# The low parts of the second layer's weights move from VectorE to GpSimd

## The reference

```python
h = x @ b_w_in[0]                                   # 1024 -> 2560
q, k, v, q_mem = jnp.split(h, [768, 1536, 2304], axis=-1)
mix = moba_attention(...)                           # 12 heads of 64, causal; one block of 256 here
mem_out = memory_cross_attention(q_mem, mem, w_mem_kv[i])
sub = jnp.concatenate([mix, mem_out], axis=-1) @ w_mix_out[i]      # 1024 -> 1024
x = layer_norm(ALPHA * x + sub, ln_mix_g[i], ln_mix_b[i])
g, u = jnp.split(x @ w_ffn_in[i], 2, axis=-1)       # 1024 -> 2 x 2816
x = layer_norm(ALPHA * x + (silu(g) * u) @ w_ffn_out[i], ln_ffn_g[i], ln_ffn_b[i])
```

## Time and profile before

| | us |
|---|---|
| median of 3 runs | 1897.1 (1896.48 to 1898.4) |
| the profiled execution, by its own time | 1896.98 |
| its span, first to last instruction | 1895.2 |
| TensorE busy (share of the span) | 1812.7 (96%) |
| VectorE busy | 788.0 (42%) |
| ScalarE busy | 571.9 (30%) |
| GpSimd busy | 17.0 (1%) |

### The profile page before, as it was taken

The page is one execution under the profiler, slowest core; times in us unless marked ns, Lnnn a source line. Parts: engine busy times, 40 slices in busy tenths (PEclk is TensorE's granted clock), DMA queues, the critical chain, the costliest instruction groups (busy, mean ns, idle before and its releaser), DMA issues. The chain is left out here.

```text
span 1895.2 us, 24227 instructions
## 1 busy us (share of the span) xinstructions
PE 1812.7 (96%) x9748; PEld 1159.7 (61%) x9748; DVE 788.0 (42%) x1161; ACT 571.9 (30%) x911; POOL 17.0 (1%) x33
## 2 busy tenths in 40 slices
PE   7999999999999999989999999999999999999998
PEld 6799888843333333334333333337888888978886
DVE  5867655511112111121121111216676656666665
ACT  4444554410101100011000110105555544645552
POOL 1000001000000000000000000000000000000000
PEclk7999999999999999999999999999999999999999
DMA  9976755899999999999999999999355556336552
GB/s 343 324 247 230 244 199 189 291 403 425 431 430 432 430 429 431 431 430 428 429 431 429 432 431 430 431 429 336 117 181 193 189 167 220 114 111 201 197 171 99
DMA packets 155403, 592.41 MB, mean 313 GB/s; under 512 B 6703, under 2 KB 85743, under 8 KB 128832
## 3 DMA queue, kind: packets, MB, share of 16 engines
q1 hardware_dynamic: 152816, 582.90, 78.3%
q0 software_dynamic: 2512, 8.45, 1.4%
HBM read 590.26 MB, written 1.07 MB: 312 GB/s over the span
## 5 line engine op out<-in xcount | busy, mean ns | idle before, releaser
L1742 PE MATMUL psum<-shared,expert_arena 128*64 128x512 f32 x1536 | 342.5, 597 | 18.8 <-DMA shared<-in_w_mlp_dram 18.7
L1595 DVE TENSOR_SCALAR expert_arena<-psum 128x512 f32<-128x512 f32 x32 | 22.1, 692 | 583.1 <-PE psum L1742 583.1
L1742 PEld LDWEIGHTS psum<-shared,expert_arena 128*64 128x64 f32 x1536 | 107.4, 137 | 237.7 <-issue 201.1
L425 PE MATMUL psum<-layer_x_parts,layer_w_hi 128*128 128x512 f32 x704 | 240.5, 396 | 0.4 <-DVE layer_x_parts L2253 0.4
L1502 ACT ACTIVATE expert_arena<-expert_arena 128x512 f32<-128x512 f32 x32 | 20.1, 630 | 561.9 <-DVE expert_arena L1595 561.9
L424 PE MATMUL psum<-layer_x_parts,layer_w_lo 128*128 128x256 f32 x616 | 171.8, 279 | 0.0
L352 DVE TENSOR_TENSOR mixer_w_lo<-mixer_ring,mixer_w_hi 128x1024 fp32r<-128x1024 f32 x96 | 116.2, 1223 | 88.9 <-ACT mixer_w_hi L347 88.4
L352 DVE TENSOR_TENSOR layer_w_lo<-slots_ahead,layer_w_hi 128x1024 fp32r<-128x1024 f32 x96 | 116.8, 1224 | 82.9 <-ACT layer_w_hi L347 82.9
L347 ACT CAST mixer_w_hi<-mixer_ring 128x1024 fp32r<-128x1024 f32 x96 | 100.0, 1048 | 153.0 <-PE psum L393 87.3
L425 PEld LDWEIGHTS psum<-layer_x_parts,layer_w_hi 128*128 128x128 f32 x704 | 125.8, 188 | 24.6 <-DVE layer_x_parts L2253 0.8
L391 PE MATMUL psum<-layer_w_hi,layer_x_parts 128*128 128x512 f32 (+1 forms) x384 | 138.9, 362 | 1.0 <-DVE layer_x_parts L2253 1.0
(11 more groups left out here) (316 smaller groups left out, 2663.5 us busy)
## 6 DMA issues: line engine op xcount, KB each, us to landing
shared<-in_w_mlp_dram SPq DMA_DIRECT2D x98, 2048.0 KB, 22.0
expert_ring<-in_w_mlp_dram SPq DMA_DIRECT2D x64, 2048.0 KB, 25.3
mixer_ring<-in_w_in_dram SPq DMA_DIRECT2D x38, 1024.0 KB, 6.3
slots_ahead<-in_w_mlp_dram SPq DMA_DIRECT2D x15, 2048.0 KB, 25.7
mixer_ring<-in_w_ada_dram SPq DMA_DIRECT2D x22, 1024.0 KB, 5.9
slots_ahead<-in_w_ffn_in_dram SPq DMA_DIRECT2D x21, 1024.0 KB, 4.9
memory_kv<-in_w_mlp_dram SPq DMA_DIRECT2D x15, 1024.0 KB, 24.7
kept<-in_w_mlp_dram SPq DMA_DIRECT2D x15, 1024.0 KB, 26.7
```

Source lines behind the costliest of these rows:

```text
L425: last = self.nc.tensor.matmul(out, hi, both[:, k].rearrange("p h s -> p (h s)"), start=k == 0, stop=k == KC - 1)
L1595: nc.vector.tensor_scalar(glu, both[:, :, 0], LIMIT, None, ALU.min).then_inc(glu_ready, 1)
L1742: last = nc.tensor.matmul(U[CAP * h:CAP * h + CAP, N * n:N * n + N], xg[:, k, j, :], expert_slot(M, k // 2)[:, at:at + N], start=False, st ...
```

## The change

In the second layer (`i = 1`) the subtraction is issued by GpSimd. Its list gets all 94 of them in a row, in the order of the units, behind its four DMA issues and ahead of its wait for them; each waits for the same `hi_ready` count and gives the same `lo_ready` signal as before. VectorE keeps its place for everything else. The first layer and the first network are as before.

```diff
+    def split_low_aside(self, pool, u):
+        raw, hi, lo = self.views(u)
+        pool.wait_ge(self.hi_ready, u + 1)
+        self.nc.gpsimd.tensor_tensor(lo, raw, hi.bitcast(FP32), ALU.subtract).then_inc(self.lo_ready, 1)
...
             for n, name in enumerate(("ln_mix_g_2", "ln_mix_b_2", "ln_ffn_g_2", "ln_ffn_b_2")):
                 pool.dma_start(rows[:, n, :].unsqueeze(1), A[name][i:i + 1, :].partition_broadcast(P)).then_inc(rows_here, 16)
+            if i:
+                for u in range(len(jobs.units)):
+                    stream.split_low_aside(pool, u)
             pool.wait_ge(rows_here, 64)
...
                 if what == "split":
                     if job == BUFFERS and i == 0:
                         final_norm()
-                    stream.split_low(dve, job)
+                    if i == 0:
+                        stream.split_low(dve, job)
                     continue
```

## The result

The changed kernel takes 1900.79 us, the kernel before 1896.74 us beside it (medians of 7 runs each): 1.0024 of its time, 95% interval 1.0015 to 1.0034. It is slower by about 4 us. I had forecast 1906.9 us, about 10 us slower. The sign was right and the time lies in the range, but the size was more than twice too large. The profiled execution took 1900.76 us by its own time, 1899.0 of them in the span.

What follows compares the result with a forecast made beforehand. TensorE was taken to bound the layer; 8.4 us for the late start plus 1.7 for the clock less 0.2 gained made 9.9 us on 1896.98, so 1906.9 us. The range ran from 1897.8 to 1920 us.

Steps and rivals of the forecast that it cites:

- step 1 of the sum: Start of the second layer: GpSimd loads for 8.7 us before its first subtraction, so TensorE starts 8.4 us later.
- the sign against it: Start of the second layer: the forecast is wrong if GpSimd's first subtraction starts by 1591 us.
- The price of one subtraction: Each low part on GpSimd: taken as 2.2 us, two passes, between bounds of 1.22 and 3.3 us.
- Step 2: Behind the layer's start: TensorE's clock falls to 1.2 GHz after standing 9.4 us, costing 1.7 us.
- the first rival: Layer start: the ISA step costs nothing or at most a table load, TensorE starts 1.0 us later, 1897.8 us; chance 0.15.
- Step 4: Output projection: GpSimd's fourth low part ends at 1689.7 us, needed at 1690.0, so hidden by 0.3 us.
- Steps 3, 5 and 6: Scores, values and projections; feed-forward layer; tail: GpSimd's work is hidden or absent there, costing nothing.
- The gain of 0.2 us: Between the two norms of the mixer's output: without VectorE's low part the eviction comes 0.2 us earlier.
- The second rival: GpSimd and VectorE collide in SBUF at two places, 1.05 and 1.4 us; both give 1909.3 us; chance 0.12.
- the upper end of 1914 us: Whole kernel: 11.0 us of loading, subtractions of 2.8, both SBUF collisions and 3.4 us for the clock.
- the third rival: From 1704 us on, GpSimd becomes the bound: 1938 us at 3.3 us a subtraction, about 1916 at 2.9; chance 0.10.

Runs made afterwards that it cites:

- e9: Changed kernel, second layer's unit 0 made first (ScalarE before casts, GpSimd before DMA issues), GpSimd's unit 28 delayed until VectorE's residual; 1.0003 of the kernel before.
- e4: Changed kernel plus one tiny GpSimd subtraction (four columns) at the start of the first layer; 1.0045 of the kernel before.
- e3: Changed kernel, but VectorE makes the low part of unit 28, between the two norms, GpSimd the other 93; 1.0010 of the kernel before.
- e7: Changed kernel, but GpSimd begins unit 28's low part only when the first tile's norm is done; 1.0015 of the kernel before.
- b1: Kernel before, with VectorE making unit 0's low part of the second layer twice, GpSimd computing nothing; 1.0020 of the kernel before.
- e6: Changed kernel with each GpSimd subtraction cut into four pieces of 256 columns; 1.0160 of the kernel before.
- e1: Changed kernel, but VectorE makes the low part of the layer's unit 0, GpSimd the other 93; 1.0006 of the kernel before.
- e8: Changed kernel with VectorE making unit 0's low part and GpSimd's unit 28 waiting until VectorE has done the residual; 1.0009 of the kernel before.
- e10: Changed kernel: unit 0's high part first, GpSimd's DMA issues behind its fourth low part, VectorE making unit 27's, unit 28 delayed; 1.0037 of the kernel before.
- e11: Like e10, but with GpSimd's four DMA issues behind its tenth low part instead of its fourth; 0.9997 of the kernel before.

## Why the prediction came out as it did

**What failed: step 1 of the sum, the price of the ISA instruction.** I had nothing that priced it and took 8.7 us, the middle of the landing times of four DMAs; it made 8.4 of the 9.9 us. It costs nothing that anyone waits for: GpSimd started 0.11 us behind its input's end, with the step 1.2 us before it, and 0.08 us in e9, with the step 1.1 us before; in e4 the step stood 0.1 us before a subtraction. The prediction had named this as the sign against it: a first subtraction by 1591. What is left of the step is the subtraction itself, +1.11. The row that fitted best, the first ISA instruction of the program with MEMSETs behind it after 0.25 us, I put aside because "that one stands before operations that are ready anyway"; this one was ready too. The Trainium skill, page "GPSIMD Engine Reference", section "2.1 Instruction dispatch", has about 6 us for the first call of a freshly loaded kernel. By that, an estimate, the first subtraction could not have started before 1588.8 + 6 = 1594.8 us; it started at 1590.04, and in e9 it was as prompt, so no such load shows in the traces; whether these runs had to load anything is not seen in a trace.

**The price of one subtraction**, 2.2 us, came out at 2.34 to 2.44, mostly 2.40; VectorE's 1.22 and three passes, 3.3, were the ends.

**Step 2, the clock, 1.7 us:** 1.49, right in size and with another cause behind it. I had tied it to a gap of 9.4 us and let the first rival's gap of 2 us pass ("leaves the clock alone"). It fell behind a gap of 2.13 us (after, e3, e7), of 2.28 (b1) and of 2.57 (e6, 13.16 to the scores), but not behind one of 2.13 in e4. Behind the gaps of 1.02 us (before, e1, e8) it stayed at 1.00.

**Step 4, the projection**, was "hidden by 0.3 us; each 0.1 us on the price beyond 2.28 costs 0.4". At 2.37 from start to start that makes 0.36; measured 0.45. The rule was right, only the price was not.

**Steps 3, 5 and 6**, no cost: right. The stretches from the scores to the projection and from the second transposes to the last matmul are unchanged to 0.01 us. e6 shows how thin the cover is: 0.4 us more a unit cost 21.5 us there.

**The gain of 0.2 us** exists (0.16 in e7) but was buried under the collision.

**The second rival, the lock in SBUF**, was right at the first of its places: I gave the second norm 1.05 us late, net of the gain; measured 1.02 net (e3 and e7 take it away). At its second place, 1626.29, nothing happened in the changed kernel, since VectorE came first (L2215 at 1628.22, the subtraction at 1628.63). The Trainium skill, page "SBUF — State Buffer", section "Who interferes with whom", says that whoever comes first holds the shared ports for a whole instruction. Within one instruction the traces agree: 2.86 and 2.91 us against 0.69, and nothing for L2224 with its PSUM input. Beyond one instruction they show more: in e6 and e10 VectorE was in some places out until GpSimd's row of instructions ended, and in others got in at the first change.

**Why the first rival did not win either.** It had the right start (+1.0) and nothing for the clock or the collision, and gave 1897.8. The measured time is a mixture that none of my cases held: free loading, the clock's fall, the collision and the pace. 1.0 + 1.7 + 1.05 on the kernel before would have been 3.75 us, next to the 4.1 measured. I had all three numbers in the text, in three separate cases; they are independent terms of one sum, each with its own chance.

**Two sums in the text do not come out**, and neither bears on the result: the upper end of 1914 us leaves out the 2.1 us that step 4 asks for at 2.8 us a subtraction, and the third rival's own formula gives 1911 us, not 1916, at 2.9.

## What to carry to other kernels

Moving work off an engine that nobody waits for gains only where it stood in someone's chain (here 0.2 us of 115), and the engine that takes it must be looked at in each place: its price per operation in the first wait, its pace against the consumer's, and whom it shuts out. An instruction with no price in the trace is bounded by the rows that resemble it, not by transfers that happen to stand near; where the bounds are 0 and 11 us, the middle is no estimate. Beside GpSimd, VectorE's instructions with two SBUF inputs should meet it idle: see that it has caught up before each one that TensorE waits for, and put its other duties, such as DMA issues, in its idle time (e11 against e10, 7.3 us). Cutting GpSimd's work into pieces did not do it (e6).

## What the runs showed of the hardware

- GpSimd's subtraction of 128 x 1024 float32 takes 2.34 to 2.44 us alone (2.37 from start to start), VectorE's 1.22; in four pieces it takes 2.78, so a piece costs some 0.13 us of its own, an estimate.
- A VectorE instruction with two SBUF inputs that is ready while GpSimd works waits at least for the end of GpSimd's instruction (2.9 us for 0.69 us of work), and sometimes for the end of its unbroken row: 7.36 us (e10) and 7.52 us (e6) for 1.23 us of work.
- Conversely GpSimd waits for VectorE's: in e11 two subtractions took 5.03 and 5.43 us instead of 4.74 in places where they overlap with one.
- The ISA step ahead of GpSimd's first subtraction cost nothing that anyone waited for: the subtraction started 0.1 us behind its input in the changed kernel and in e9, and took 0.52 us for four columns in e4.
- TensorE's clock fell to 0.50 behind idle times of 2.13 us in three traces and not in a fourth; each fall ahead of the first product cost 1.4 to 1.5 us. Behind 5.6 us (e10) and 5.8 us (e6) of idle time it cost an estimated 1.6 and 2.6 us.
